# Interleaving the two halves of a matmul's moving row, in runs of 2 to 128 columns

## The reference

```python
y = jax.nn.gelu(y.reshape(bsz, s, SSM_WIDTH)).astype(u.dtype)
return y * jax.nn.sigmoid(y @ w_glu + b_glu)                    # s5_branch: y_ssm
...
merged = (jax.nn.sigmoid(gate_a) * (y_attn @ w_attn_br[l])
          + jax.nn.sigmoid(gate_s) * (y_ssm @ w_ssm_br[l]))
x = x + g1[:, None] * (merged @ w_out[l])
```

## Time and profile before

| | us |
|---|---|
| median of 3 runs | 3577.97 |
| lowest, highest | 3575.41, 3583.42 |
| span of the profiled execution, first to last instruction | 3572.0 |
| PE matmul busy in it | 3530.3 (99%) |
| PE weight load busy | 3340.6 (94%) |
| VectorE busy | 2650.0 (74%) |
| ScalarE busy | 2076.8 (58%) |
| mean granted TensorE clock | 0.998 |

### The profile page before, as it was taken

One profiled execution on the slowest core, in us unless ns is written; L12 is line 12 of the kernel. 1 busy time (PEld: TensorE's weight loads), 2 busy tenths in 40 slices (PEclk: granted clock), 3 DMA queues, 4 the chain that ended last, 5 costly groups with the idle time before them and its releaser, 6 DMA issues.

```text
span 3572.0 us, 75102 instructions
## 1 busy us (share of the span) xinstructions
PE 3530.3 (99%) x26786; PEld 3340.6 (94%) x26786; DVE 2650.0 (74%) x4903; ACT 2076.8 (58%) x3860; POOL 104.1 (3%) x169
## 2 busy tenths in 40 slices
PE   7999999999999999999999999999999999999999
PEld 6999999999999999787788889999999999999999
DVE  7875687688888888555688877998657686666555
ACT  5455655677767777455455556664565565555554
POOL 1000020000000000000000000000000000000000
PEclk9999999999999999999999999999999999999999
DMA  8854487455555555565788874554455555556555
GB/s 308 328 192 144 148 295 277 149 187 183 186 177 165 165 164 162 163 215 187 265 329 329 329 246 139 171 160 155 145 180 185 183 184 183 187 183 186 185 185 173
DMA packets 184770, 721.33 MB, mean 202 GB/s; under 512 B 20512, under 2 KB 23072, under 8 KB 171808
## 3 DMA queue, kind: packets, MB, share of 16 engines
q1 hardware_dynamic: 167328, 608.57, 52.5%
q0 software_dynamic: 14496, 103.82, 8.2%
q10 hardware_dynamic: 2784, 6.78, 0.5%
HBM read 714.89 MB, written 4.19 MB: 201 GB/s over the span
## 4 chain that ended last, share of the span: by engine, by line
PE 96%; DVE 3%; ACT 1%; DMA 1%; issue 0%; SPq 0%; DVEq 0%; ACTq 0%
PE PS L444 24%; PE PS L446 23%; PE PS L445 23%; PE PS L583 7%; PE PS L584 6%; PE PS L585 6%; PE PS L804 1%; PE PS L850 0%; PE PS L669 0%; DMA raw<-peer_v_dram 0%; DVE big L1562 0%; PE PS L596 0%; DVE wlo L1492 0%; PE PS L779 0%; PE PS L617 0%
## 5 line engine op out<-in xcount | busy, mean ns | idle before, releaser
L444 PE MATMUL PS<-hhi,whi 128*128 128x256 f32 (+1 forms) x6208 | 1758.9, 283 | 13.2 <-DVE hlo L1553 10.5
L445 PE MATMUL PS<-hlo,whi 128*128 128x256 f32 (+1 forms) x6208 | 1751.2, 282 | 0.0
L446 PE MATMUL PS<-hhi,wlo 128*128 128x256 f32 (+1 forms) x6208 | 1750.4, 282 | 0.0
L989 ACT ACTIVATE whi<-raw 128x512 fp32r<-128x512 f32 x1832 | 1139.8, 629 | 1045.3 <-PE PS L446 690.7
L1492 DVE TENSOR_TENSOR wlo<-raw,whi 128x512 fp32r<-128x512 f32 x1448 | 976.2, 690 | 578.5 <-ACT whi L989 573.8
L444 PEld LDWEIGHTS PS<-hhi,whi 128*128 128x128 f32 x6208 | 1174.0, 189 | 25.6 <-issue 22.2
L446 PEld LDWEIGHTS PS<-hhi,wlo 128*128 128x128 f32 x6208 | 1175.0, 189 | 0.0
L445 PEld LDWEIGHTS PS<-hlo,whi 128*128 128x128 f32 x6208 | 1167.9, 188 | 0.6
L1623 DVE TENSOR_TENSOR wlo<-raw,whi 128x512 fp32r<-128x512 f32 x596 | 409.0, 700 | 167.4 <-ACT whi L1077 113.7
L1077 ACT ACTIVATE whi<-raw 128x512 fp32r<-128x512 f32 x468 | 292.6, 630 | 292.3 <-PE PS L446 290.5
L583 PE MATMUL PS<-whi,hhi 128*128 128x512 f32 x1024 | 403.9, 394 | 3.9 <-issue 2.2
(11 more groups left out here) (463 smaller groups left out, 3391.9 us busy)
## 6 DMA issues: line engine op xcount, KB each, us to landing
raw<-peer_u_dram SPq DMA_DIRECT2D x256, 512.0 KB, 3.5
raw<-peer_v_dram SPq DMA_DIRECT2D x256, 512.0 KB, 4.2
raw<-w_in_dram SPq DMA_DIRECT2D x240, 512.0 KB, 3.6
big<-w_mod_dram POOLq DMA_DIRECT2D x96, 1024.0 KB, 5.3
raw<-w_up_dram SPq DMA_DIRECT2D x176, 512.0 KB, 3.5
raw<-w_down_dram SPq DMA_DIRECT2D x88, 512.0 KB, 3.5
raw<-w_out_dram SPq DMA_DIRECT2D x64, 512.0 KB, 3.6
raw<-w_query_dram SPq DMA_DIRECT2D x32, 512.0 KB, 4.5
```

Source lines behind the costliest of these rows:

```text
L444: pe.matmul(out, hi, rhi, start=start, stop=False, **more)
L445: pe.matmul(out, hi, rlo, start=False, stop=False, **more)
L446: return pe.matmul(out, lo, rhi, start=False, stop=stop, **more)
L989: f(whi[:, m % PAIRS, quarter(q)], raw[:, m % RING, quarter(q)], ACT.Copy).then_inc(hi_ready, 1)
```

## The change

`dense_turn` and `dense_half` get an argument `run`. A new helper `woven` rewrites a row of 256 columns, for the moving operand and for the sums in `PS` alike: the row is cut into two halves of 128 columns (`a`), each half into pieces of `run` columns (`c`), and the order becomes piece 0 of the first half, piece 0 of the second half, piece 1 of the first, and so on. Each column's sum still goes to its own place. Without `run` nothing is rewritten.

```diff
-            def dense_turn(name, chunk0, width, g, after=None, inputs=None, halves=None, shift=0, tiles=None):
+            def dense_turn(name, chunk0, width, g, after=None, inputs=None, halves=None, shift=0, tiles=None, run=None):
...
-                                last = three(PS[:, (c + shift) % 4, 0:width], whi[:, half, at_], wlo[:, half, at_], hi[:, kc, :], lo[:, kc, :],
+                                last = three(woven(PS[:, (c + shift) % 4, 0:width], run), whi[:, half, at_], wlo[:, half, at_],
+                                             woven(hi[:, kc, :], run), woven(lo[:, kc, :], run),
                                              half == 0 and kc == 0, half == 1 and kc == 7)
...
-            def dense_half(name, chunk0, base, hi=hhi[:, :, META:], lo=hlo[:, :, META:]):
+            def woven(v, run):
+
+                return v if run is None else v.rearrange("p (a b c) -> p b a c", a=2, c=run)
+
+            def dense_half(name, chunk0, base, hi=hhi[:, :, META:], lo=hlo[:, :, META:], run=None):
...
-                            last = three(PS[:, (c + 2) % 4, 0:SEQ], whi[:, c % 2, at_], wlo[:, c % 2, at_],
-                                         hi[:, base + kc, :], lo[:, base + kc, :], kc == 0, kc == 7)
+                            last = three(woven(PS[:, (c + 2) % 4, 0:SEQ], run), whi[:, c % 2, at_], wlo[:, c % 2, at_],
+                                         woven(hi[:, base + kc, :], run), woven(lo[:, base + kc, :], run), kc == 0, kc == 7)
...
-            dense_half("w_glu", 280, 0, ysh, ysl)
+            dense_half("w_glu", 280, 0, ysh, ysl, run=64)
             pe.wait_ge(in_ready, SPLITS["ya"])
-            dense_half("w_attn_br", 288, 8)
+            dense_half("w_attn_br", 288, 8, run=128)
             pe.wait_ge(in_ready, SPLITS["ys"])
-            dense_half("w_ssm_br", 304, 0)
+            dense_half("w_ssm_br", 304, 0, run=32)
             for g in range(4):
                 dense_turn("w_out_2", 320, SEQ, g, None, SPLITS["ys"] if g == 0 else None,
-                           ((hhi[:, 8:, META:], hlo[:, 8:, META:]), (mhi, mlo)), shift=2)
+                           ((hhi[:, 8:, META:], hlo[:, 8:, META:]), (mhi, mlo)), shift=2, run=(2, 4, 8, 16)[g])
```

## The result

| | before | changed |
|---|---|---|
| median, us | 3579.38 | 3590.94 |
| lowest to highest | 3575.41 to 3583.42 | 3584.05 to 3591.88 |
| runs | 9 | 9 |
| span of the profiled execution | 3572.0 | 3589.7 |

The ratio over all runs is 1.0031, 95% interval 1.0022 to 1.0039; the medians are 11.6 us apart. The wider range, 3571 to 3603, held the time, by the part of it that stood there for rivals 1 and 2.

A forecast was written before the change was run, and what follows sets the result against it. PE's matmuls were taken to bound the kernel, with nothing hiding a slower one. Issue and stream at 0 added 0 to a 3572.0 us span, and 6.0 around it gave 3578 us; range 3571 to 3603, the forecast's own 3572 to 3585.

The forecast's parts named there:

- Rival 1: In w_out_2's first turn, runs of two columns go at half pace: +18.4 us, 3596 us; chance 0.20.
- Rival 2: In all woven rows, each jump costs the stream about one column's time, 0.45 ns: +21.8 us, 3600 us; chance 0.13.
- its own sign: In the changed kernel's profile: the prediction is wrong if any turn of w_out_2 is more than 2 us longer.
- What bounds the kernel: In the four products from w_glu to w_out_2, PE matmuls alone set the time; their pitch, 119 ns, counts one to one.
- Issue at 0: In the woven matmuls, taking in a pattern with one more dimension stays hidden within the 119 ns pitch: 0 us.
- The stream at 0: In the woven matmuls, jumps in the moving rows and sums cost the stream nothing: 0 us.
- Where I was least sure: w_out_2's first turn, runs of two: 192 matmuls, 22.8 us; partly used fetches might cost there, but 0 was taken.
- Rival 3: In w_glu, w_ssm_br and w_out_2, every woven row goes at half pace, 215 ns: +129 us, 3707 us; chance 0.07.
- Rival 4: In the woven products, new address order avoids what makes `mhi` rows 3 ns dearer than `hhi`: 4 us faster, 3574; chance 0.02.

## Why the prediction missed

The number of the forecast missed by 13 us, and by its own sign the prediction was wrong: one turn is 9.1 us longer where 2 was the bound. That the wide range held is due to its rivals, not to the forecast.

- *What bounds the kernel* held in full: PE busy throughout, the price one to one in the time, the others with more room.
- *Issue at 0* held: runs of 64, whose pattern has as many dimensions as any, cost nothing.
- *The stream at 0* is the step that failed: it put the runs of two at +0 ns per matmul, and they cost +47.3, all of it on the reading side (+7.9 at runs of 4). I argued that a plain row shows one even price per column and that stepping an outer dimension on VectorE is no event. Both are true and neither bears on a run of two. By the account with two walks, the plain row already uses just half of what each walk fetches, which would be why it takes 119 ns where 111.7 is possible; no row of the trace before could show that.
- *Where I was least sure* was right: the first turn of w_out_2, for the reason given (a part of each fetch used, and back for the rest). It has 9.1 of the 12 us and passes the bound that rival 1 was given, 38 ns, with 47.
- *Rival 1* came nearest, with the runs of two as the dear ones, and was mis-sized: half pace was priced at +96 ns from the f32 row, and it was +47. The chance of 0.20 was too low, that of no change too high. About half pace (218 to 233 ns) is what pairs from four and more places cost, which the change does not have; why two places cost less is open.
- *Rival 2*, a stair, was there as well, at a fraction of its price: 0.37 ns a jump at 2 columns and some 0.1 from 4 columns up, not 0.45. (48576 x 0.45 is 21.9 us, not 21.8.)
- *Rival 3*, every woven row at 215 ns, fell with the changed kernel itself, where five of the six widths are within 8 ns of a plain row; the kernel that only wrote woven showed no price on the side of the sums at all.
- *Rival 4*, faster, was wrong for this change and right in kind: the order of reading can gain, and by 7.5 ns rather than 3. The reason it gave, the addresses of `mhi` against `hhi`, was not what the runs bore out.

## What to carry to other kernels

Read a matmul's price from start to start, and compare it with the shortest pitch of its shape anywhere: 119 against 112 ns for 256 fp32r columns was a gain of 3% of this kernel that lay open. For fp32r moving rows keep runs at whole, aligned groups of four columns, avoid pairs from places eight or more columns apart, and try two halves read one column at a time, left in that order in PSUM and put right by the engine that reads them. When a test changes distance and number of places together it answers neither; change one.

## What the runs showed of the hardware

- A woven fp32r row costs on the reading side alone: +47.3, +7.9, +3.9, +0.9 ns per 256 columns at runs of 2, 4, 8 and 16; woven writing costs 0 at each.
- Pairs of fp32 columns: 164 to 168 ns from two places 8 to 128 columns apart, 186 from three places (252 columns), 218 to 233 from four and more, 111.8 from two places 4 apart.
- Aligned groups of four fp32 columns count as one: runs of four begun two columns into a group cost 167 ns, on its edge 123 (248 columns).
- Two halves read a column at a time: 111.7 ns for 256 columns where plain rows take 118 to 120, and 215 for 512 where they take 233.
- bf16 rows of 128 columns: 69 to 70 ns at runs of 2, 56 to 59 at runs of 4, where plain ones take 56.
- VectorE reads every second column of the sums at no added time (479 against 478 ns).
